# An expert layer's weight subtraction taken off GpSimd, and gate times sigmoid as one activation function

## The reference, cut to what matters

```python
def expert_block(args):
    idx, e = args
    xb = t[idx]                                   # 128 tokens' rows
    hu = xb @ w1[e] + b1[e]                       # 1024 -> 2048
    glu = jnp.minimum(hu[:, 0::2], SWIGLU_LIMIT)
    lin = jnp.clip(hu[:, 1::2], -SWIGLU_LIMIT, SWIGLU_LIMIT)
    act = glu * jax.nn.sigmoid(SWIGLU_ALPHA * glu) * (lin + 1)
    return act @ w2[e] + b2[e]                    # 1024 -> 1024
```

## Time and profile before

| | |
|---|---|
| Median of 3 runs | 3359.65 us (3359.26 to 3365.08) |
| The profiled execution | 3360.82 us |
| Its span, first to last instruction | 3359.2 us |
| Mean granted TensorE clock over the span | 0.944 of full speed |
| PE busy, share of the span | 2876.1 us, 86% |
| DVE busy | 1903.3 us, 57% |
| ACT busy | 1400.2 us, 42% |
| POOL busy | 831.9 us, 25% |

### The profile page before, as it was taken

How to read it: one execution, slowest core, us unless ns; L and a number is a source line. 1 busy time by engine, 2 the same in 40 slices (tenths; PEclk the granted TensorE clock), 3 DMA queues, 4 the chain that set the end, 5 groups by cost and what they waited for, 6 DMA issues and landing times. The chain is left out here.

```text
span 3359.2 us, 40318 instructions
## 1 busy us (share of the span) xinstructions
PE 2876.1 (86%) x13206; PEld 2162.3 (64%) x13207; DVE 1903.3 (57%) x2864; ACT 1400.2 (42%) x1667; POOL 831.9 (25%) x609
## 2 busy tenths in 40 slices
PE   4899979998957707999999999999999999999980
PEld 0254667777734405777777777777777777777760
DVE  0430024454422256677767776866776687667786
ACT  0100125555521105445544554554455455545551
POOL 1000021212211143224322322332232233323340
PEclk8999989999978858999999999999999999999995
DMA  9700032323132108568657766775676577667678
GB/s 248 252 26 25 13 94 56 77 49 87 45 105 75 75 8 308 211 219 300 229 209 262 266 229 225 267 267 207 225 287 230 219 275 256 222 228 281 241 284 312
DMA packets 285165, 629.36 MB, mean 187 GB/s; under 512 B 9922, under 2 KB 11202, under 8 KB 284962
## 3 DMA queue, kind: packets, MB, share of 16 engines
q1 hardware_dynamic: 261558, 549.12, 47.7%
q0 software_dynamic: 23568, 79.73, 6.6%
HBM read 584.63 MB, written 50.26 MB: 189 GB/s over the span
## 5 line engine op out<-in xcount | busy, mean ns | idle before, releaser
L1311 DVE TENSOR_TENSOR w_lo_x<-wring_x,w_hi_x 128x2048 fp32r<-128x2048 f32 (+1 forms) x422 | 885.1, 2145 | 118.5 <-PE psum L1404 113.1
L1256 ACT ACTIVATE w_hi_x<-wring_x 128x2048 fp32r<-128x2048 f32 x424 | 787.8, 1909 | 148.9 <-DMA wring_x<-in_w_mlp 148.7
L1402 PE MATMUL psum<-w_hi_x,x_hi_x 128*128 128x512 f32 x1632 | 676.4, 414 | 8.5 <-DVE w_lo_x L1311 8.5
L1404 PE MATMUL psum<-w_hi_x,x_lo_x 128*128 128x512 f32 x1632 | 637.2, 390 | 0.0
L1403 PE MATMUL psum<-w_lo_x,x_hi_x 128*128 128x512 f32 x1632 | 637.0, 390 | 0.0
L1208 POOL TENSOR_TENSOR w_lo_x<-wring_x,w_hi_x 128x512 fp32r<-128x512 f32 x212 | 312.9, 1480 | 864.0 <-ACT w_hi_x L1256 464.6
L1402 PE MATMUL psum<-w_hi_x,a_hi_x 128*128 128x512 f32 x816 | 346.2, 424 | 51.9 <-DVE a_lo_x L1321 50.3
L1402 PEld LDWEIGHTS psum<-w_hi_x,x_hi_x 128*128 128x128 f32 x1632 | 308.4, 189 | 69.6 <-DVE w_lo_x L1311 10.6
L1404 PEld LDWEIGHTS psum<-w_hi_x,x_lo_x 128*128 128x128 f32 x1632 | 306.9, 188 | 65.9
L1403 PEld LDWEIGHTS psum<-w_lo_x,x_hi_x 128*128 128x128 f32 x1632 | 307.7, 189 | 62.2
L1403 PE MATMUL psum<-w_lo_x,a_hi_x 128*128 128x512 f32 x816 | 322.1, 395 | 0.0
(11 more groups left out here) (249 smaller groups left out, 3535.6 us busy)
## 6 DMA issues: line engine op xcount, KB each, us to landing
wring_x<-in_w_mlp SPq DMA_DIRECT2D x212, 2048.0 KB, 8.2
ring<-in_w_ada SPq DMA_DIRECT2D x12, 2048.0 KB, 9.5
bias<-bias_d SPq DMA_DIRECT2D x16, 1280.0 KB, 14.2
yg<-y_d SPq DMA_DIRECT2D x8, 2048.0 KB, 10.4
ring<-in_w_in SPq DMA_DIRECT2D x4, 2048.0 KB, 9.6
xin<-in_x SPq DMA_DIRECT2D x8, 512.0 KB, 5.1
ring<-in_w_out SPq DMA_DIRECT2D x2, 2048.0 KB
mix_d<-o SPq DMA_DIRECT2D x8, 512.0 KB, 6.6
```

Source lines behind the costliest of these rows:

```text
L1256: act.activation(w_hi[:, n % HI, k, :], ring[:, n % RING, k, :], ACT.Copy).then_inc(hi_done, 1)
L1311: dve.tensor_tensor(w_lo[:, n % LO, k, :], ring[:, n % RING, k, :], w_hi[:, n % HI, k, :].bitcast(F32), ALU.subtract).then_inc(lo_done, 1)
L1402: pe.matmul(bank, hi[:, r, k, :], w_hi[:, n % HI, k, :], start=False, stop=False)
L1404: last = pe.matmul(bank, lo[:, r, k, :], w_hi[:, n % HI, k, :], start=False, stop=(k == KD - 1))
```

## The change

POOL no longer takes part in the subtraction: DVE's second half covers k = 4 to 7, and the semaphore `pool_lo_done`, with the waits of SP and PE on it, is gone. ACT computes Silu of `ALPHA * glu` in place of the sigmoid. DVE's step `lin = (lin + 1) * glu` and its wait for itself are gone, and the last step computes `(lin + 1) * sig`. The result is ALPHA times too large; the factor 1 / ALPHA is applied where the transposed piece is read from PSUM, in ACT's copy (as its scale) and in DVE's subtraction (as the scalar of a scalar_tensor_tensor).

```diff
@@ -1089,7 +1089,6 @@
     HI, LO = 3, 2
     PAIRS = UNIT // 2
     KC = KD // CH
-    KP = KD - 1
     RMAX = 2
     ctx = ExitStack()
     with ctx:
@@ -1111,14 +1110,13 @@
         bias_loaded = sem("bias_loaded")
         w_loaded = [sem(f"w_loaded{r}") for r in range(RING)]
-        hi_done, lo_done, pool_lo_done, prod_done = sem("hi_done"), sem("lo_done"), sem("pool_lo_done"), sem("prod_done")
+        hi_done, lo_done, prod_done = sem("hi_done"), sem("lo_done"), sem("prod_done")
         record_loaded, gathered, gate_open = sem("record_loaded"), sem("gathered"), sem("gate_open")
         xt_done, xhi_done, x_ready = sem("xt_done"), sem("xhi_done"), sem("x_ready")
         sel_up_ready, sel_down_ready = sem("sel_up_ready"), sem("sel_down_ready")
         glu_done, sig_done, up_free, act_done = sem("glu_done"), sem("sig_done"), sem("up_free"), sem("act_done")
         at_done, ahi_done, a_ready = sem("at_done"), sem("ahi_done"), sem("a_ready")
         y_copied, y_stored, y_free = sem("y_copied"), sem("y_stored"), sem("y_free")
-        dve_own = sem("dve_own")
         block = ctx.enter_context(nc.Block())
@@ -1158,7 +1156,6 @@
                 if not isinstance(split_before, int):
                     split_before = sp.snap(split_before)
                 sp.wait_ge(lo_done, split_before)
-                sp.wait_ge(pool_lo_done, split_before)
                 src = w1[bass.ds(e, 1), :, :, n * UNIT:(n + 1) * UNIT] if n < UP else w2[bass.ds(e, 1), :, :, (n - UP) * UNIT:(n - UP + 1) * UNIT]
                 sp.dma_start(ring[:, n % RING, :, :], src.rearrange("a p k n -> (a p) k n")).then_inc(w_loaded[n % RING], 16)
@@ -1203,42 +1200,25 @@
             def gate():
                 pool.tensor_tensor(poolgate[:, 1:2], poolgate[:, 0:1], poolgate[:, 0:1], ALU.add).then_inc(gate_open, 1)
-            def split(unit, n):
-                pool.wait_ge(hi_done, CH * unit + CH)
-                pool.tensor_tensor(w_lo[:, n % LO, KP:, :], ring[:, n % RING, KP:, :], w_hi[:, n % HI, KP:, :].bitcast(F32), ALU.subtract).then_inc(pool_lo_done, CH)
-
-            pool.sem_inc(pool_lo_done, RING * CH)
             pool.wait_ge(gathered, 16)
-            split(0, 0)
-            split(1, 1)
             def body(st, next_r):
                 nxt = st.then(next_r)
-                unit = NU * st.passes
                 pool.wait_ge(gate_open, 3 * st.passes + 2)
                 pool.tensor_tensor(y_row[:, 0:st.R], record[:, 0:st.R, 1], int_zero[:, 0:st.R], ALU.add).then_inc(gate_open, 1)
                 pool.wait_ge(gate_open, 3 * st.passes + 3)
                 load_record(nxt)
-                pool.wait_ge(prod_done, units_done(st, 1))
-                split(unit + 2, 2)
                 pool.wait_ge(record_loaded, 16 * st.passes + 32)
                 pool.wait_ge(xt_done, st.blocks + st.R)
                 gate()
                 gather(next_r)
-                for n in range(3, NU):
-                    pool.wait_ge(prod_done, units_done(st, n - 1))
-                    split(unit + n, n)
-                pool.wait_ge(prod_done, units_done(st, NU - 1))
-                split(unit + NU, 0)
                 pool.wait_ge(gathered, 16 * (st.blocks + st.R + next_r))
                 pool.wait_ge(gate_open, 3 * st.passes + 4)
                 pool.wait_ge(y_copied, DOWN * (st.blocks + st.R) + 2)
                 gate()
                 for r in range(st.R):
                     pool.indirect_dma_start(K.y_d, bass.IndirectOffsetOnAxis(ap=y_row[:, r:r + 1], axis=0), y[:, r, :], None).then_inc(y_stored, 16)
-                pool.wait_ge(prod_done, units_done(st, NU))
-                split(unit + NU + 1, 1)
                 pool.wait_ge(y_stored, 16 * (st.blocks + st.R))
                 pool.sem_inc(y_free, 1)
@@ -1262,7 +1242,7 @@
             def columns(st, j):
                 act.wait_ge(at_done, UP * st.blocks + j + 1)
                 n, r = divmod(j, st.R)
-                act.activation(a_hi[:, r, 2 * n:2 * n + 2, :].rearrange("p k n -> p (k n)"), ps[:, 2 + j % 2, 0:2 * P], ACT.Copy).then_inc(ahi_done, 1)
+                act.activation(a_hi[:, r, 2 * n:2 * n + 2, :].rearrange("p k n -> p (k n)"), ps[:, 2 + j % 2, 0:2 * P], ACT.Copy, scale=1.0 / ALPHA).then_inc(ahi_done, 1)
             first = Step(1, 0, 0)
             rows(first, 0)
@@ -1283,7 +1263,7 @@
                     if n < UP:
                         for j in range(n * st.R, n * st.R + st.R):
                             act.wait_ge(glu_done, UP * st.blocks + j + 1)
-                            act.activation(sig[:, j % 2, :], glu[:, j % 2, :], ACT.Sigmoid, scale=ALPHA).then_inc(sig_done, 1)
+                            act.activation(sig[:, j % 2, :], glu[:, j % 2, :], ACT.Silu, scale=ALPHA).then_inc(sig_done, 1)
                             if j:
                                 columns(st, j - 1)
                         continue
@@ -1306,7 +1286,7 @@
             def split(unit, n):
                 for c in range(CH):
-                    k = slice(KC * c, min(KC * (c + 1), KP))
+                    k = slice(KC * c, KC * (c + 1))
                     dve.wait_ge(hi_done, CH * unit + c + 1)
                     dve.tensor_tensor(w_lo[:, n % LO, k, :], ring[:, n % RING, k, :], w_hi[:, n % HI, k, :].bitcast(F32), ALU.subtract).then_inc(lo_done, 1)
@@ -1318,8 +1298,8 @@
             def columns(st, j):
                 dve.wait_ge(ahi_done, UP * st.blocks + j + 1)
                 n, r = divmod(j, st.R)
-                dve.tensor_tensor(a_lo[:, r, 2 * n:2 * n + 2, :].rearrange("p k n -> p (k n)"), ps[:, 2 + j % 2, 0:2 * P],
-                                  a_hi[:, r, 2 * n:2 * n + 2, :].bitcast(F32).rearrange("p k n -> p (k n)"), ALU.subtract).then_inc(a_ready, 1)
+                dve.scalar_tensor_tensor(a_lo[:, r, 2 * n:2 * n + 2, :].rearrange("p k n -> p (k n)"), ps[:, 2 + j % 2, 0:2 * P], 1.0 / ALPHA,
+                                         a_hi[:, r, 2 * n:2 * n + 2, :].bitcast(F32).rearrange("p k n -> p (k n)"), ALU.mult, ALU.subtract).then_inc(a_ready, 1)
             def select(sel, e, ready):
@@ -1335,7 +1315,6 @@
             def body(st, next_r):
                 nxt = st.then(next_r)
                 unit = NU * st.passes
-                link = linker(dve, dve_own, UP * st.blocks)
                 e, e_next = expert_of(dve, st), expert_of(dve, nxt)
                 for n in range(NU):
                     if n == UP:
@@ -1356,9 +1335,8 @@
                             dve.tensor_scalar(glu[:, s, :], pairs[:, :, 0], LIMIT, None, ALU.min).then_inc(glu_done, 1)
                             dve.tensor_scalar(lin[:, s, :], pairs[:, :, 1], LIMIT, -LIMIT, ALU.min, ALU.max).then_inc(up_free, 1)
                             dve.wait_ge(up_free, UP * st.blocks + j + 3)
-                            link(dve.scalar_tensor_tensor(lin[:, s, :], lin[:, s, :], 1.0, glu[:, s, :], ALU.add, ALU.mult))
                             dve.wait_ge(sig_done, UP * st.blocks + j + 1)
-                            dve.tensor_tensor(act_o[:, s, :], lin[:, s, :], sig[:, s, :], ALU.mult).then_inc(act_done, 1)
+                            dve.scalar_tensor_tensor(act_o[:, s, :], lin[:, s, :], 1.0, sig[:, s, :], ALU.add, ALU.mult).then_inc(act_done, 1)
                             if j:
                                 columns(st, j - 1)
                         if n == UP - 1:
@@ -1366,7 +1344,6 @@
                     elif n == UP:
                         for r in range(1, next_r):
                             rows(nxt, r)
-                assert link.count[0] == UP * st.R
             program(dve, body)
@@ -1395,8 +1372,6 @@
                     if r == 0:
                         pe.wait_ge(lo_done, CH * unit + c + 1 + RING * CH)
                     for k in range(KC * c, KC * (c + 1)):
-                        if r == 0 and k == KP:
-                            pe.wait_ge(pool_lo_done, CH * unit + CH + RING * CH)
                         if ready:
                             ready(k)
                         pe.matmul(bank, hi[:, r, k, :], w_hi[:, n % HI, k, :], start=False, stop=False)
```

## The result

The changed kernel takes 3527.01 us (median; 3524.32 to 3528.05) against 3360.86 for the kernel before on the same chip: ratio 1.0491, interval 1.0473 to 1.0509. The forecast was 3338, the range 3321 to 3357. The profiled execution took 3526.2 us with a span of 3524.5, 165.3 more than the span before.

A forecast was written before the change was run, and what follows sets the result against it. PE was taken to bound the kernel. Long a_lo waits -16, w_lo -2, gather's chain -3.5 and first pass -0.5 made -22 us from 3360.8, so 3338.8, set to 3338 against the median; range 3321 to 3357.

The forecast's parts named there:

- What bounds the stage: Expert stage: PE bounds it, busy 1874 of 1999.5 us; the change is worth at most PE's waits.
- the 17.7 us of long a_lo waits: PE's 14 waits before the third activation piece in singles, from POOL delaying DVE; -16 us booked.
- rival C: The long a_lo wait comes from DVE's queue length, so it stays: 3357 us; chance 0.10.
- Steps 2 to 4: DVE and ACT: longer split half +0.53 us a unit, one multiply-add less, Silu and scaled reads at equal cost.
- rival B: ACT's tables: if Silu's set had no Copy, every piece would switch, costing 142 us: 3480; chance 0.03.
- Step 5: SP's load loses its wait on POOL: load 4 leaves some 3 us earlier, easing ACT, inside the 17.7 us.
- The gather's term, -3.5: Gather's chain on POOL: small ops start 0.45 us earlier in 16 singles, 7 us, halved for loads running beside it.
- Rival A: The gather lands later, beside earlier loads and behind longer DVE halves; rows at 28.3 us, time 3379; chance 0.07.
- The clock, ±3 us: TensorE's clock: one fall to 1.2 GHz costs 1.6 us; the number of falls may differ by two either way.
- The shared port: POOL's two small ops in the gather's chain could be caught behind DVE's longer halves: up to 17 us lost.

The follow-up runs named there:

- e8: e5 with POOL's gates (a 128x1 add) turned into memsets: 3325.40 us, ratio 0.9894.
- e11: e8 with two buffers for the destination rows, so record load and gather need not wait for the row stores to land: 3318.06 us, ratio 0.9873.
- e1: The kernel before with only the activation edits (Silu, one multiply less, factor at the transposed read): 3353.35 us, ratio 0.9972.
- e5: The changed kernel with POOL memsets behind row stores, record load and gather, which SP waits for before load 4, load 5 and the next load 0: 3364.44 us.
- e7: The kernel before, all work kept, with POOL's subtraction of unit 1 moved from behind the row stores to ahead of them: 3482.97 us, ratio 1.0362.
- e3: The changed kernel with a counter POOL raises, without arithmetic, where its subtractions stood; SP waits for it before loads: 3484.81 us, ratio 1.0353.

## Why the prediction was wrong

*What bounds the stage; the 17.7 us of long a_lo waits:* right. They were POOL's collisions with DVE and they are gone to the last one, against rival C. In the changed kernel PE's long wait for rows could have hidden them, but e8, whose rows wait is shorter (17.7) than before, has the same 32.6. Only where rows hardly wait at all (e11) does the length of DVE's queue show, with 6.9 us. act_o takes 0.426 on average in the stage (0.641 before), every split half 2.28, and a clean split 4.48 against 4.49 predicted.

*Steps 2 to 4 (longer half, one multiply less, Silu):* right. The table loads stay at 16 on each of the two lines, against rival B, and e1 shows the activation edits to be a gain of 0.28%.

*Step 5, SP's load loses its wait on POOL:* this is the step that failed. It found that load 4 would leave "some 3 us earlier", which it did (5.0 instead of 8.0), and booked that as a relief for ACT. The relief did not come: ACT waited 2.98 us for that load instead of 2.52. And the step never asked what POOL did in those 3 us. My own sentence had it: "two row stores and the subtraction came behind" the gate. The subtraction's place in POOL's queue, behind each of three small transfers, was what kept the load behind them. e5 gives the order back and recovers 163 of 166 us; e7 takes it from the kernel before, with all work kept, and loses 122. By what mechanism a load in flight holds the small transfers up (shared bandwidth or the order in which requests are served) no run here tells.

*The gather's term, -3.5:* the wrong sign, +170.4. I halved a gain because "the loads now run earlier beside the gather" instead of working that out on the chain store, record, gather, in which each leg waits for the landing of the one before. Rival A named the gather and the point where it decides (rows later than 26.8), but saw only the last leg and priced rows at 28.3; they came at 35.3, and its chance was 0.07. The evidence I held against A, that two kinds of single have the same 25.2, said nothing: both had the loads in the same order. Nor was the rest of the term right: with the order back, e5 still has rows 26.2 above the kernel before, and that is about the distance from the forecast of 3338 to its 3364.

*The clock, ±3 us:* mis-sized. PE's wait of 11.7 us put the rows' transposes and the start of unit 4 of each such single at the lower level, 20 us of PE time in all.

*The shared port:* the Trainium skill's page "SBUF — State Buffer", section "Who interferes with whom", says that a DVE instruction with two SBUF inputs contends with a GpSimd instruction that reads SBUF. The trace agrees for the gates: the chain's second gate took 1.29 us where it had 0.66, and as a memset, which reads nothing, it takes 0.10 (e8). The gather's first issue took 2.89 where 2.35 stood. Together that is about 1 us of the 10 in a single.

## What to carry to other kernels

Before a wait is removed, list what the releasing instruction stands behind in its own queue: a wait on cheap work can be the only thing that orders two kinds of transfers. Where a large prefetch has slack and a small transfer is on a chain, the prefetch should leave second, and the order should hang on an operation that is counted when it is done. A transfer chain must be priced leg by leg, with the landing of each under the load that will then be in flight.

## What the runs showed of the hardware that was not expected

- In the changed kernel, where load 4 leaves while a single's row stores are being issued, a store takes 9.7 us from issue to landing (median of 51) instead of 4.7.
- The load gained nothing by going first: it left 3 us earlier and was there 0.5 us later (ACT's copy at 16.5 instead of 16.0 us into the single).
- A counter raised by POOL's program without an operation ran ahead of an indirect DMA that stands before it: load 4 left at 2021.59, the second store was issued from 2022.58 to 2023.55 (e3). One raised by a memset did not: the memset ended at 1991.47, the load left at 1991.74 (e5).
- The issue of an indirect DMA on POOL ends 0.87 us behind the end of DVE's split in both kernels: it took 2.33 beside a split that ended at 1987.22 and 2.86 beside one that ended at 2033.35; away from a split it took 0.97. In e8 it ended 0.86 behind (1974.79 and 1973.93). So DVE's tensor_tensor seems to hold it up too. A memset is not held up: e8's gate took 0.10 at 1970.06, in the middle of DVE's split (1969.44 to 1973.93).
